# State-space blocks: a block's output products stand in the next block's first product, their turn back in its third, and the output maps follow the phases

## The reference, cut to what matters

```python
s_re = einsum('btgh,gph->btgp', u_g, bb_re)      # and s_im
x    = associative_scan(_combine, (a, s), reverse=reverse, axis=1)
y    = einsum('btgp,ghp->btgh', x_re, c_re) - einsum('btgp,ghp->btgh', x_im, c_im)
ys   = y(direction 0) + y(direction 1) + ssm_d * u
```

```python
p = h_x @ w_in                                   # xa, ba, ca, za are 1024 columns each
v = ca * xa
ya = ba * short_conv(v, w) * silu(za)            # then @ proj_a
```

## Time and profile before

| | us |
|---|---|
| time, median of 3 runs (2119.87 to 2121.78) | 2119.97 |
| the profiled execution's own time | 2119.78 |
| its span | 2118.0 |
| TensorE busy in the span | 2051.6 (97%) |
| TensorE weight loads (overlap the matmuls) | 1667.9 (79%) |
| VectorE busy | 1086.1 (51%) |
| ScalarE busy | 586.1 (28%) |
| TensorE's waits for `M` before the output products, 8 in all | 7.7 |

### The profile page before, as it was taken

One profiled execution on the slowest core, in us unless ns is written; L12 is line 12 of the kernel. 1 busy time (PEld: TensorE's weight loads), 2 busy tenths in 40 slices (PEclk: granted clock), 3 DMA queues, 4 the chain that ended last, 5 costly groups with the idle time before them and its releaser, 6 DMA issues.

```text
span 2118.0 us, 26445 instructions
## 1 busy us (share of the span) xinstructions
PE 2051.6 (97%) x9915; PEld 1667.9 (79%) x9915; DVE 1086.1 (51%) x1596; ACT 586.1 (28%) x816; POOL 27.3 (1%) x16
## 2 busy tenths in 40 slices
PE   3999999999999999999999999999999999999996
PEld 0578888888888788888888888888588888888885
DVE  5445898888888545554333444332343333333333
ACT  4325233333333322222222222222122222222231
POOL 0003100000000000000000000000000000000000
PEclk9999999999999999999999999999999999999998
DMA  9873533343333544443334444444033333334423
GB/s 371 309 217 112 171 101 100 92 104 98 104 99 108 165 125 141 128 136 106 99 97 134 141 131 125 126 132 146 10 94 95 100 99 91 97 99 158 169 93 116
DMA packets 384830, 272.16 MB, mean 128 GB/s; under 512 B 24804, under 2 KB 349900, under 8 KB 382916
## 3 DMA queue, kind: packets, MB, share of 16 engines
q1 hardware_dynamic: 374416, 267.04, 40.9%
q10 hardware_dynamic: 10356, 4.35, 1.5%
HBM read 253.25 MB, written 18.09 MB: 128 GB/s over the span
## 4 chain that ended last, share of the span: by engine, by line
PE 80%; DVE 9%; DMA 4%; ACT 2%; ACTq 2%; issue 2%; SPq 0%; DVEq 0%
PE ac L704 20%; PE ac L705 20%; PE ac L708 20%; ACTq L1090 2%; DVE S L1549 2%; DMA M<-Tl 1%; PE ss L879 1%; PE ac L878 1%; PE ac L879 1%; PE ss L880 1%; PE ac L880 1%; PE ss L878 1%; ACT S L894 1%; DMA wslot<-w_in 1%; PE ac L845 1%
## 5 line engine op out<-in xcount | busy, mean ns | idle before, releaser
L1448 DVE TENSOR_TENSOR wlo<-wslot,whi 128x1024 fp32r<-128x1024 f32 x310 | 379.6, 1225 | 647.9 <-ACT whi L894 643.8
L894 ACT ACTIVATE whi<-wslot 128x1024 fp32r<-128x1024 f32 x328 | 347.1, 1060 | 1253.2 <-PE ac L708 1034.4
L704 PE MATMUL ac<-hxh,whi 128*128 128x512 f32 x1664 | 652.3, 392 | 0.0
L705 PE MATMUL ac<-hxl,whi 128*128 128x512 f32 x1664 | 648.0, 389 | 0.0
L708 PE MATMUL ac<-hxh,wlo 128*128 128x512 f32 x1664 | 411.1, 389 | 0.9 <-DVE wlo L1448 0.9
L704 PEld LDWEIGHTS ac<-hxh,whi 128*128 128x128 f32 x1664 | 312.4, 188 | 67.8 <-issue 3.1
L708 PEld LDWEIGHTS ac<-hxh,wlo 128*128 128x128 f32 x1664 | 312.3, 188 | 66.1 <-DVE wlo L1448 1.3
L705 PEld LDWEIGHTS ac<-hxl,whi 128*128 128x128 f32 x1664 | 312.5, 188 | 64.3 <-issue 0.2
L704 PE MATMUL ac<-bah,whi 128*128 128x512 f32 x384 | 149.4, 389 | 0.0
L705 PE MATMUL ac<-bal,whi 128*128 128x512 f32 x384 | 149.4, 389 | 0.0
L708 PE MATMUL ac<-bah,wlo 128*128 128x512 f32 x384 | 94.8, 389 | 0.0
(11 more groups left out here) (316 smaller groups left out, 2135.7 us busy)
## 6 DMA issues: line engine op xcount, KB each, us to landing
wslot<-w_in SPq DMA_DIRECT2D x224, 512.0 KB, 3.9
ring<-w_ada SPq DMA_DIRECT2D x64, 512.0 KB, 8.0
gwt<-w_ada SPq DMA_DIRECT2D x128, 128.0 KB, 2.4
wslot<-w_out SPq DMA_DIRECT2D x32, 512.0 KB, 3.6
wslot<-proj_a SPq DMA_DIRECT2D x16, 512.0 KB, 4.1
wslot<-proj_b SPq DMA_DIRECT2D x16, 512.0 KB, 4.0
wslot<-proj_c SPq DMA_DIRECT2D x16, 512.0 KB, 3.9
xn<-x SPq DMA_DIRECT2D x4, 1024.0 KB, 8.8
```

The lines of the kernel that those rows point to most:

```text
L704: mm(ac[:, bank, :], w, xh, start=(v == 0 and q == 0), stop=False)
L705: mm(ac[:, bank, :], w, xl, start=False, stop=False)
L894: cp = lambda o, i, scale=1.0: nc.scalar.activation(o, i, ACT.Copy, scale=scale)
L1448: tt(wlo[:, s, :], wslot[:, s, :], whi[:, (U0[k] + j) % 2, :].bitcast(F32), ALU.subtract)\
```

## The change

On TensorE the output products become a function `y_products(b)`; in all blocks but the first it is called as `mid` of the first product, so they come behind unit 0 of the next block, not behind unit 7 of their own. The turn back `y_back(b)` moves from `mid` of the first product to `mid` of the third, behind unit 4. The last block's output products and turn back follow the loop. On ScalarE `y_cols` goes behind `hi` of unit 2 and `y_rows` behind `hi` of unit 6. On VectorE the phases and the diagonal's scale move ahead of `lo` of unit 2, and the output maps and their adds follow, one `lo` later each than before. On SyncE the store of the outputs goes from behind load 4 to behind load 7. No instruction is added or dropped other than waits.

SyncE:

```diff
-                    if k == 1 and j == 4 and not (isinstance(i, int) and i == 0):
+                    if k == 1 and j == 7 and not (isinstance(i, int) and i == 0):
                         y_store(i - 1)
```

TensorE:

```diff
+        def y_products(b):
+            pe.wait_ge(t_add, 1)
+            pe.wait_ge(t_add, b)
+            pe.wait_ge(x_done, b)
+            pe.wait_ge(m_in, b * 128)
+            for g in range(GB):
+                o = ss[0:NX, g // 4, (g % 4) * 128:(g % 4 + 1) * 128]
+                mm(o, U[:, g, NC:NQ], M[:, g, :], start=True, stop=False)
+                mm(o, X[:, 0, g // 2, g % 2, :], Cp[:, 0, g, H:(L + 1) * H], start=False, stop=False)
+                last = mm(o, X[:, 1, g // 2, g % 2, :], Cp[:, 1, g, 0:L * H], start=False, stop=True)
+            last.then_inc(y_ps, 1)
...
-            product(1, b, 0, 2, 0, xs_of, mid=None if first else (lambda: y_back(b)))
+            product(1, b, 0, 2, 0, xs_of, mid=None if first else (lambda: y_products(b)))
             pe.wait_ge(v_done, b + 1)
+            if not first:
+                pe.wait_ge(yt_cp, b)
             for d in range(2):
-                if d and not first:
-                    pe.wait_ge(yb_cp, b)
...
-            product(1, b, 4, 2, 2, xs_of)
+            def turned_output():
+                pe.wait_ge(yt_cp, 1)
+                pe.wait_ge(s_cp, 2 * b + 2)
+                y_back(b)
+            product(1, b, 4, 2, 2, xs_of, mid=None if first else turned_output)
...
             product(1, b, 6, 2, 3, xs_of)
-            pe.wait_ge(t_add, b + 1)
-            pe.wait_ge(x_done, b + 1)
-            pe.wait_ge(m_in, b * 128 + 128)
-            for g in range(GB):
...
-            last.then_inc(y_ps, 1)
-
         repeat(pe, NB, conv_turn, peel=1)
+        y_products(NB)
         y_back(NB)
```

ScalarE:

```diff
+            hi(1, b, 2)
             if not first:
                 y_cols(b)
-            hi(1, b, 2)
-            if not first:
-                y_rows(b)
             hi(1, b, 3)
...
             hi(1, b, 6)
+            if not first:
+                y_rows(b)
             hi(1, b, 7)
```

VectorE:

```diff
             if dyn or b:
+                dve.wait_ge(a_done, b)
+            phases(b)
+            tt(dd[:, :, :], ident[0:H, 0:H].unsqueeze(1).to_broadcast([H, GB, H]),
+               dtab[0:H, sl(b, GB)].unsqueeze(2).to_broadcast([H, GB, H]), ALU.mult)
+            lo(1, b, 2)
+            if dyn or b:
                 dve.wait_ge(y_ps, b)
             for d in range(2):
...
             link(last)
-            lo(1, b, 2)
+            lo(1, b, 3)
             for d in range(2):
                 o = Cp[:, d].rearrange("p g m -> p (g m)")
                 last = tt(o, o, t1[:, d * 1152:(d + 1) * 1152], ALU.add)
             last.then_inc(cp_done, 1)
-            lo(1, b, 3)
             dve.wait_ge(cp_done, b + 1)
-            phases(b)
-            tt(dd[:, :, :], ident[0:H, 0:H].unsqueeze(1).to_broadcast([H, GB, H]),
-               dtab[0:H, sl(b, GB)].unsqueeze(2).to_broadcast([H, GB, H]), ALU.mult)
             lo(1, b, 4)
```

## The result

| | before | after |
|---|---|---|
| median, us (5 runs each) | 2119.97 | 2131.34 |
| lowest and highest | 2119.44, 2121.78 | 2130.24, 2132.61 |
| ratio, 95% interval | | 1.0053 (1.0038 to 1.0068) |
| profiled execution's own time | 2119.78 | 2132.08 |
| its span | 2118.0 | 2130.3 |

A forecast was written before the change was run, and what follows sets the result against it. TensorE, busy 2051.6 of 2118.0 us, was taken as the bound; 1.5 for block 0, plus 6 x 0.9 for the passages, less 0.1 in the last block, gave 6.8 on 2119.97: 2126.8 us, range 2120.5 to 2131.

The forecast's parts named there:

- What bounds the kernel, and the output products' new place: TensorE bounds; between blocks the 1.07 us wait for M goes, late whi and wlo of unit 8 stall it 1.97 us.
- 0.05 for the semaphore: Passage between blocks: 0.05 us added to the ready times of whi and of wlo of unit 8.
- The 50 ns: Dispatch price per DMA for ScalarE's eight issues, 0.4 us in all; the trace's 5.53 us was used instead.
- The turn back behind unit 4: Ahead of the K products: unit 7 ends 0.9 us later; Tl's copies, t_add and unit 8's split come 0.78 later.
- VectorE's new order, "hidden": Phases ahead of wlo of unit 2: TensorE wants that wlo some 5 us later, so it costs nothing.
- SyncE's queue, the store behind load 7, put at "Nothing": The store holds the next block's first load back by 2 us, with 10 us of room: no cost.
- shrinks by 0.1: Last block: M shifts by 0.78 and unit 7 by 0.9, so the 1.4 us wait for M shrinks by 0.1.
- Rival C: SyncE's load of unit 4 lands late behind u_load, 1 us in each of seven blocks: 2133.8 us; chance 0.07.
- The forecast's own bounds: Stalls of 1.7 to 2.4 us per block, 0.6 to 1.3 more per block: 2124.8 to 2129.5 us.
- A: Passages between blocks: unit 8's split is on time, only the wait for M goes: 2112.5 us; chance 0.13.
- B: Turn back behind unit 4 delays unit 7 but not t_add: 0.1 more per block, 2121.4 us; chance 0.13.
- D: The wait for M is not removed, M being late by 5.4 us more; chance under 0.01.

The follow-up runs named there:

- both halves first: Changed kernel with VectorE's wlo of unit 8 ahead of the next input maps and ScalarE's whi of unit 8 ahead of the turned tables: 2117.75 us, ratio 0.9984.
- seventh run: Changed kernel with the fourier_w copies issued ahead of the output store, and whi and wlo of unit 8 ahead of tables and maps: 2115.86 us, ratio 0.9975.

## Why the prediction was right or wrong

The forecast of the loop's blocks was right, in mechanism and nearly in size; what it had wrong lies in the last block, where it put a moved store at nothing, and in block 0.

*What bounds the kernel, and the output products' new place*: right. The wait for `M` went, and `whi` and `wlo` of unit 8 were late. The forecast for the seven passages was 1.5 + 6 x 0.9 = 6.9 us; they measure 6.92. This is partly luck: the six are 1.04 each (58.62 against 57.58), and the first is 0.66, since block 0's own loss had taken part of its stall (with block 0 in the old order the first passage is 1.79 longer than before). The size of the stalls was right: a block takes 58.62 us, and 56.63 with both halves first, so the stalls are 1.99 where 1.97 stood, and 0.05 for the semaphore, which had no row behind it, is 0.06 from the end of `wlo` (588.98) to the matmul. What was read too large is what the edit gives back: the gap before is 57.58 - 56.63 = 0.95 over six blocks, not the 1.07 of the one block shown. The 50 ns that the prediction took from the Trainium skill, "DMA: Bandwidth & Descriptors", stand there in "Anatomy of one DMA — SWDGE (gpsimd) path", a table for DMAs issued from GpSimd, so they were no price for ScalarE's; the eight take 5.26 us after the change, and going by the trace was right.

*The turn back behind unit 4*: right. VectorE waits 0.70 us for `Tl`, as worked out (0.78). It delays `t_add` and unit 7 alike, and that it costs nothing of its own is shown by the runs with the products in their own block (57.5 us a block).

*VectorE's new order, "hidden"*: right in blocks 1 to 7, wrong in block 0. The step took its start from the end of `Abr`, and block 0 has no `Abr` of a block before: VectorE comes straight from the input maps, with no slack. The 1.33 us there stood at nothing. Only 0.1 of them are a loss in the changed kernel, by the run with the old order; in the kernel without a wait at the passage they are 1.3.

*SyncE's queue, the store behind load 7, put at "Nothing"*: this step failed, and with it the last block's "shrinks by 0.1". It looked at the next block's first load, and in the last block what stands behind the store are the two copies of `fourier_w`. The last wait for `M` grew by 1.34 us, and the clock fell behind it for another 1.41: 2.75 us where -0.1 stood. The copies are the cause by three runs: copies early in the changed kernel (wait 0.81), copies early with the products in their own block (1.11 instead of 2.70), and copies late in the kernel before (3.20 instead of 1.42). The Trainium skill, "DMA: Bandwidth & Descriptors", says in "Issuing engines are not separate DMA queues" that DMAs of the scalar and sync engines run on the same 16 DMA engines and interleave; the traces agree, as SyncE's copies stretch ScalarE's `M` from 4.65 to 6.42 us to landing in the kernel before, and to 5.92 in the changed one, where it is 4.00 with the copies early. Rival C named this queue, but at the load of unit 4, which was never waited for.

*The clock* had no term at all: 1.41 us in the profiled execution, right behind the longer wait. The Trainium skill, "TensorE: Matmul & The Clock Gate", gives in "What's actually happening" 1.2 and 2.4 GHz as the two states, and the distances of 0.44 and 0.22 us agree.

*The sum*: 6.8 forecast, 11.4 measured by the medians, 12.3 between the two profiled executions. Of the 12.3, 11.0 lie where the change acts: 6.9 in the passages, 1.3 in block 0, 1.3 for the late `M`, 1.4 for the clock. Set against the forecast's terms, the six passages took 0.9 more than forecast (6.26 against 5.4), block 0 and the first passage 0.5 more (1.33 and 0.66 against 1.5), the last `M` 1.4 more and the clock 1.4. The remaining 1.3 are the part before the loop and the end (0.98 and 0.29). The forecast's own bounds of 2124.8 to 2129.5 come out at 2125.0 to 2129.2 from its terms; the missing 2.75 at the loop's end is more than either leaves room for. The later series of the kernel before had medians of 2120.3 to 2121.2, so the first comparison may have put it about 1 us low; this stays open within the interval of 8 to 14.4 us.

*Rivals.* A (the gap closes) fell: L704 and L708 wait. B fell: VectorE waits for `Tl`. D fell: `M` is not waited for in blocks 0 to 6. The sign named for C, ScalarE waiting for `wslot<-w_in`, did show once at the loop's end (10.47 us), from the store and the copies and not from the loads of `U`, and cost TensorE nothing.

## What to carry to other kernels

Work that fills an engine while it waits is also a cover for what comes next: ahead of moving it, read when each operand of the instruction that moves up is ready, and move the operands' makers in the same edit. When an instruction is moved past a point in a queue, look at that queue in the first and last turns of the loop too, where other work stands behind it. A saving ahead of a chain that another engine sets is waited for behind it, so an edit that measures nothing can have its worth once that chain is shorter.

## What the runs showed of the hardware

A wait of TensorE of about 3 us can cost half as much again in the clock. Of the six kernels whose last wait for `M` was 2.4 to 3.2 us, four (2.77, 3.10, 2.70 and 3.20) had the granted clock at half for part of the matmuls behind it, at once or, with 3.10, a microsecond on, at a cost of 1.4 to 1.7 us; two (2.45 and 2.71) did not. In the six whose last wait was 0.8 to 1.4 us it did not fall there. At 2.70 and 2.71 us it went both ways, so the length of the wait alone does not decide it.

A second place shows the same. Behind a wait of 1.83 us for `fT`, later in the program, the profiled execution with both halves first (the fourth run) has its next 32 matmuls in 8.83 us, at half the clock for the first of them, and the kernel before, behind the same 1.83 us, in 7.14:

```profile
1482.57 8.83 PE L837 MATMUL ss<-dftw,fT 128*128 128x256 f32 x32 [1.83 <-ACT fT L902]
```

```profile
1486.29 7.14 PE L829 MATMUL ss<-dftw,fT 128*128 128x256 f32 x32 [1.83 <-ACT fT L894]
```

The seventh run's profile has 8.83 there too. That is 1.7 us which no edit here aimed at, as much as some of the differences between these kernels, so a difference of 1 or 2 us between two profiled executions is read stretch by stretch.
